# Moving norms, step sizes, a bias table and loads inside a two-block sequence model on one core

## What is computed

```python
h = rms_norm(x, norm_g[l]); proj = h @ w_in[l]
z, xbc, dt_raw, lru_gate, lru_x, q, gate_logits = jnp.split(proj, SPLIT_POINTS, axis=-1)
xbc = jax.nn.silu(causal_dwconv(xbc, ssd_conv_w[l], ssd_conv_b[l]))
dt = jax.nn.softplus((dt_raw + ssd_dt_bias[l]).astype(jnp.float32))
mem_n = rms_norm(mem, mem_norm_g[l])           # keys and values of the memory attention
# second block: x = x + rmsnorm(mixer(rmsnorm(x, pre_norm[i])), post_norm[i]) for S5, SWA, MLA, SGU
bias = rel_bias[t5_bucket(jnp.maximum(dist, 0))]   # SWA only
```

## Time and profile before

| what | us |
|---|---|
| median of three timed runs (2287.07 to 2291.01) | 2290.78 |
| the profiled execution, its own time | 2285.02 |
| span of the profiled execution | 2283.2 |
| PE busy in it | 2060.8 |
| DVE, ACT, POOL busy | 1276.0, 873.3, 483.9 |

### The profile page before, as it was taken

The page is one execution under the profiler, slowest core; times in us unless marked ns, Lnnn a source line. Parts: engine busy times, 40 slices in busy tenths (PEclk is TensorE's granted clock), DMA queues, the critical chain, the costliest instruction groups (busy, mean ns, idle before and its releaser), DMA issues.

```text
span 2283.2 us, 25052 instructions
## 1 busy us (share of the span) xinstructions
PE 2060.8 (90%) x10096; PEld 1601.8 (70%) x10096; DVE 1276.0 (56%) x1807; ACT 873.3 (38%) x1262; POOL 483.9 (21%) x394
## 2 busy tenths in 40 slices
PE   5899998999999998999998888979879988898986
PEld 3687776678757887768797666857667755567865
DVE  5887666634729342455445534466476365637383
ACT  4225555422159223422332243335532344444332
POOL 3961221132238600423300100011001001100001
PEclk9899999999999999999999999989989999999998
DMA  2242111133422432624545622621122301113311
GB/s 115 82 155 99 38 38 37 65 106 110 143 92 93 148 111 88 226 82 130 176 131 137 149 74 74 116 89 42 70 79 74 110 20 37 37 58 119 110 56 55
DMA packets 53138, 215.26 MB, mean 94 GB/s; under 512 B 6048, under 2 KB 23104, under 8 KB 32672
## 3 DMA queue, kind: packets, MB, share of 16 engines
q1 hardware_dynamic: 22896, 162.54, 20.4%
q0 software_dynamic: 9488, 35.94, 5.6%
q10 hardware_dynamic: 20640, 15.19, 3.0%
HBM read 196.14 MB, written 17.50 MB: 94 GB/s over the span
## 4 chain that ended last, share of the span: by engine, by line
PE 61%; DVE 11%; ACT 6%; issue 4%; DMA 1%; ACTq 1%; POOL 0%; DVEq 0%; PEldq 0%; POOLq 0%
PE bank L480 17%; PE bank L481 17%; PE bank L482 17%; PE bank L479 2%; DVE ring_low L442 1%; ACT ring_high L437 1%; PE bank L3038 1%; ACT swa_s L2945 1%; PE bank L3065 1%; PE bank L1854 1%; ACTq L2325 1%; DVE lru_x L1768 1%; DVE swa_s L2883 1%; DVE gated_low L2745 1%; PE bank L613 1%
## 5 line engine op out<-in xcount | busy, mean ns | idle before, releaser
L480 PE MATMUL bank<-h_high,ring_high 128*128 128x512 f32 x1248 | 507.5, 407 | 50.6 <-DVE h_low L1282 22.2
L442 DVE TENSOR_TENSOR ring_low<-ring,ring_high 128x2048 fp32r<-128x2048 f32 x136 | 333.2, 2451 | 362.7 <-ACT ring_high L437 362.6
L481 PE MATMUL bank<-h_low,ring_high 128*128 128x512 f32 x1248 | 494.6, 396 | 0.0
L482 PE MATMUL bank<-h_high,ring_low 128*128 128x512 f32 x1248 | 493.2, 395 | 0.0
L437 ACT ACTIVATE ring_high<-ring 128x2048 fp32r<-128x2048 f32 x145 | 277.3, 1913 | 533.4 <-PE bank L482 497.9
L480 PEld LDWEIGHTS bank<-h_high,ring_high 128*128 128x128 f32 x1248 | 239.9, 192 | 127.7 <-issue 48.0
L481 PEld LDWEIGHTS bank<-h_low,ring_high 128*128 128x128 f32 x1248 | 240.0, 192 | 52.0 <-issue 3.9
L482 PEld LDWEIGHTS bank<-h_high,ring_low 128*128 128x128 f32 x1248 | 239.5, 192 | 51.8
L480 PE MATMUL bank<-gated_high,ring_high 128*128 128x512 f32 x256 | 106.0, 414 | 25.1 <-issue 18.3
L442 POOL TENSOR_TENSOR ring_low<-ring,ring_high 128x2048 fp32r<-128x2048 f32 x9 | 43.1, 4791 | 305.3 <-ACT ring_high L437 305.3
L481 PE MATMUL bank<-gated_low,ring_high 128*128 128x512 f32 x256 | 103.7, 405 | 0.0
(11 more groups left out here) (518 smaller groups left out, 3963.9 us busy)
## 6 DMA issues: line engine op xcount, KB each, us to landing
ring<-slabs SPq DMA_DIRECT2D x149, 1024.0 KB, 4.8
s_outputs<-s_ca POOLq DMA_DIRECT2D x4, 1152.0 KB, 4.9
x<-xT SPq DMA_DIRECT2D x2, 2048.0 KB, 8.3
s_b<-s_br POOLq DMA_DIRECT2D x8, 512.0 KB, 4.3
s_rows<-s_powers POOLq DMA_DIRECT2D x16, 256.0 KB, 6.6
s_inputs<-s_w POOLq DMA_DIRECT2D x8, 512.0 KB, 3.1
s_ck<-s_outputs POOLq DMA_DIRECT2D x1, 4096.0 KB, 23.5
s_wv<-s_inputs ACTq DMA_DIRECT2D x8, 512.0 KB, 4.9
```

The source lines that it names most:

```text
L442: dve.tensor_tensor(self.ring_low[:, s % RING, :], self.ring[:, s % RING, :], self.ring_high[:, self.splits_before[s] % AHEAD, :].bitcast( ...
L480: pe.matmul(out, w[0], x[0], start=start, stop=False)
L481: pe.matmul(out, w[0], x[1], start=False, stop=False)
L482: return pe.matmul(out, w[1], x[0], start=False, stop=stop)
```

## The change

Eight pieces of work move; no arithmetic is dropped. First norm: squares are gathered on DVE and summed by one pair of matmuls, right when x has landed; the two first slab splits go between its steps; scaling, high and low parts go one k behind another on ACT and DVE alone, without POOL. The S5 coefficients move behind the norm. The dt tile and the first three tiles are made with k outermost in four banks. The step sizes' `log1p_small` moves behind tile 4's convolution and the sums behind tile 9's. The memory norm runs beside the q tiles. `load_kernels` moves up in `stage_s5_u`, and `evac_z` goes to the end of its own step. `swa_bias` moves into S5's `gated_output`. In the MLA entry `total` takes the pinned bank 7.

```diff
-    add("dt", tile("w_in", KD, np.r_[span(C_DT, SSD_H), np.full(P - SSD_H, -1)]))
-    for m in range(24):
+    for k in range(KD):
+        add("xbc", [("w_in", span(k * P), np.r_[span(C_DT, SSD_H), np.full(P - SSD_H, -1)])])
+        add("xbc", [("w_in", span(k * P), span(C_XBC + m * P)) for m in range(3)])
+    for m in range(3, 24):
...
 stage_load, scalar
-            act.wait_ge(cols.sem, cols.base + 16)
-            s5_act(act)
+            act.wait_ge(C.consts.sem, C.consts.at(0))
+            act.activation(C.eps8[:, 6:7], C.eps[:], ACT.Sqrt)
             act.wait_ge(loaded.sem, loaded.base + 16)
-            for s in range(AHEAD):
-                C.make_high(act, s)
...
 stage_xbc, vector
-            norm.on_dve(dve)
-            norm.finish(dve)
+            for i in range(KD):
+                norm.gather(dve, i)
+            C.make_low(dve, 0)
+            norm.parts_on_dve(dve, {3: lambda dve: C.make_low(dve, 1)})
+            norm.done(dve, KD - 1)
+            for _, use in ends:
+                C.split_low(dve, use)
+            s5_dve(dve)
...
+            C.split_low(dve, us[-1])
...
-                C.split_low(dve, u)
+                if i >= 3:
+                    C.split_low(dve, u)
+                if i == 4:
+                    step_sizes()
+                if i == 9:
+                    step_sums()
 stage_xbc, scalar
-            norm.on_act(act)
-            C.split_high(act, dt[0])
+            for i in range(KD):
+                norm.square(act, i)
+            C.make_high(act, 0)
+            norm.root_on_act(act)
+            C.make_high(act, 1)
+            norm.highs_on_act(act)
+            for _, use in ends:
+                C.split_high(act, use)
+            s5_act(act)
+            C.split_high(act, us[-1])
...
 Norm, new
+    def parts_on_dve(self, dve, between={}):
...
+        scale(0)
+        for i in range(n):
+            if i + 1 < n:
+                scale(i + 1)
+            dve.wait_ge(self.highs.sem, self.highs.at(i))
+            dve.tensor_tensor(self.pair.tile(i)[1], self.tmp[i], self.pair.tile(i)[0].bitcast(F32), ALU.subtract)\
+                .then_inc(self.parted.sem, 1)
+            if i in between:
+                between[i](dve)
...
 stage_gemm (beside=mem_norm in the q stage; on PE: sum_total after tile 4)
+                if beside and i < 4:
+                    beside.square(act, 2 * i)
+                    beside.square(act, 2 * i + 1)
+                if beside and i == 4:
+                    beside.root_on_act(act)
+                if beside and i == 5:
+                    beside.highs_on_act(act)
...
+                if beside and i == 4:
+                    beside.parts_on_dve(dve)
...
 stage_s5_u, scalar
                 if half == 1:
+                    act.wait_ge(kept.sem, kept.base + 16)
+                    for b in range(2):
+                        loads.load_kernels(act, b)
                     C.split_high(act, us[-1])
...
 stage_s5_scan, vector
-            evac_z(0)
...
-                if s + 1 < NB:
-                    C.split_low(dve, z[s + 1][0])
-                    evac_z(s + 1)
+                    if s > 0:
+                        C.split_low(dve, z[s][0])
+                    evac_z(s)
...
 swa_bias(C, L, free), now a side of S5's gated_output
     def pool_part(pool):
+        C.full(pool, free)
...
-    return Side({3: product}, pool=pool_part, act={3: copy}, dve_last=lambda dve: dve.wait_ge(s.sem, s.base + 32))
+    L.bias_laid = s
+    return Side({1: product}, pool=pool_part, act={1: copy})
 stage_swa, vector
+            dve.wait_ge(L.bias_laid.sem, L.bias_laid.base + 32)
...
 branch_mla
+    total = C.take_given(7)
     qn = Norm(C, latents[:6], lambda i: C.col("q_norm", i), 768, C.take_given(7), pair=QP, early=True)
```

More of the change, by code:

```diff
@@ L686, in stage_xbc @@
     nc = C.nc
-    dt = C.take_tile(KD)
-    tiles = [C.take_tile(KD) for _ in range(24)]
+    us = [C.take_bank() for _ in range(4)]
+    blocks, ends = [], []
+    for k in range(KD):
+        use = us[-1]
+        if k < KD - 1 and C.block_no % SLAB + 4 >= SLAB:
+            C.midway += 1
+            use = SlabSpent(C.midway)
+            ends.append((k, use))
+        blocks.append(C.take_blocks(4, use))
+    tiles = [(u, None) for u in us[1:]] + [C.take_tile(KD) for _ in range(21)]
+    s5_act, s5_dve = s5_coefficients(C)
     tables = Tables(C, L, items)
@@ L708, in _ @@
             seen = set()
-            norm.on_pe(pe)
-            C.gemm(pe, dt, C.H.tiles(KD), seen, ready=lambda k: norm.done(pe, k))
-            for t in tiles:
+            norm.sum_total(pe)
+            for u in us:
+                C.open(pe, u)
+            for k in range(KD):
+                norm.done(pe, k)
+                for u, (s, i) in zip(us, blocks[k]):
+                    C.wait_slab(pe, s, seen)
+                    mm = C.product(pe, C.bank[u.b][:], C.block(s, i), C.H.tile(k), k == 0, k == KD - 1)
+                    if k == KD - 1:
+                        mm.then_inc(C.bank_full[u.b], 1)
+                if k in dict(ends):
+                    mm.then_inc(C.slab_spent, 1)
+            for t in tiles[3:]:
                 C.gemm(pe, t, C.H.tiles(KD), seen)
@@ L1106, with __init__ @@
 class Norm:
-    def __init__(self, C, src, g, dim, bank, root=0, pair=None, keep=False, add=None, early=False, after=None, w=T, total=2, prior=None, split=False):
+    def __init__(self, C, src, g, dim, bank, root=0, pair=None, keep=False, add=None, early=False, after=None, w=T, total=2, prior=None, split=False, alone=False):
         self.C, self.src, self.g, self.dim, self.u = C, src, g, dim, bank
@@ L1127, in __init__ @@
             self.highs = C.reserve("highs", n)
-        if (pair is not None or add is not None) and not split:
+        if (pair is not None or add is not None) and not split and not alone:
             self.last_steps()
@@ L1354, in times_root, with stage_entry @@
         return evac
-def stage_entry(C, entry, nt, evac, engine="scalar", by_token=True, then=None, stats=(), side=None):
+def stage_entry(C, entry, nt, evac, engine="scalar", by_token=True, then=None, stats=(), side=None, total=None):
     side = side or Side()
@@ L2462, in _ @@
                         loads.load_outputs(act, b)
-            act.wait_ge(kept.sem, kept.base + 16)
-            for b in range(2):
-                loads.load_kernels(act, b)
     return loads, [us for us, _, _ in halves], first_z
```

163 lines of the change are left out of this document (93 added, 70 removed).

## The result

Median 2256.36 us (2253.57 to 2264.15, four runs) against 2288.93 (2286.05 to 2291.01) for the kernel before on the same chip: ratio 0.9865, 95% interval 0.9848 to 0.9881. That is 32.6 us less by the medians; the span of the profiled execution fell by 28.8 us, to 2254.4. The forecast was 38.5 us, 2252.

A forecast was written before the change was run, and what follows sets the result against it. PE, busy 90% of the span, was taken as the bound, so time is gained only where it waits or runs at low clock. Terms 8.5 + 11.5 + 5.5 + 12 - 7 + 8 = 38.5 us off median 2290.8 give 2252, range 2236 to 2271.

The forecast's parts named there:

- the xbc stretch gives all back: Rival, 15%: slow slab split beside POOL and tables 5 us late leave parts 1 and 2 only 0 to 3; 2260.
- 1. start, first h matmul: First norm: earlier squares and sums let the first h matmul start at 24.7 instead of 34.36, 9.6 us earlier.
- 1 and 2, at the states: Start and step sizes up to stage_ssd: 9.5 us gained by tile 9, about 1 lost to POOL's tables; 8.5 (3 to 11).
- 3. memory norm: Norm beside the q tiles: memory keys start at 895.5 instead of 903.33; 11.5 us gained (9 to 14).
- 4. S5 loads and copies: S5 branch: kernel loads moved up and z copies moved later shorten PE's waits; 5.5 us gained (2 to 9).
- 5. bias table, gain at the scores: SWA scores: bias ready some 50 us ahead, so DVE's and PE's waits for it go; 12 us gained.
- 5. bias table, loss at S5's output: S5's gated output: the 3 MB write delays slab 99 and the norm's sum; 7 us lost (0 to 9).
- 6. MLA total: MLA entry: tile 5's bank is free, so PE's 4.96 us wait and low clock go; 8 us gained (5 to 8).
- a stall above 15 us: Sign of being wrong: the step sizes' stall in the xbc stretch exceeds 15 us.
- the bias write at a place with less slack: Sign of being wrong: the moved bias write hits a place with less slack than assumed.
- The step sizes' stall: xbc stretch: the old 10 us wait comes back as about 11.5 us at tile 9, with 2.8 us of low clock.
- the forecast case (2240 to 2262): Whole kernel: time lands between 2240 and 2262 us, given 61%.

The follow-up runs named there:

- e5: The changed kernel with POOL's last table of stage_xbc (outputs 1) moved to the LRU stage: 2245.4 us, ratio 0.981 to the kernel before.
- e9: The changed kernel with the memory norm put back behind the q tiles, step by step: 2270.0 us, ratio 0.9925 to the kernel before.
- e10: The changed kernel with load_kernels and evac_z back where they were: 2254.6 us, ratio 0.9859 to the kernel before.
- e8: The changed kernel with swa_bias back in the SWA entry: 2260.0 us, ratio 0.9886 to the kernel before.
- e4: The changed kernel with the 3 MB bias write cut into eight pieces, each waited for: 2247.4 us, ratio 0.9817 to the kernel before.
- e11: The changed kernel with total taking the next bank again in the MLA entry: 2264.1 us, ratio 0.989 to the kernel before.
- e2: The changed kernel with log1p_small and the sums cut into nine pieces behind splits from tile 4 to 20: 2254.2 us, ratio 0.9848 to the kernel before.
- e1: The changed kernel with the S5 coefficients computed in stage_load while x is in flight: 2257.0 us, ratio 0.9843 to the kernel before.
- e3: The changed kernel with both early S5 coefficients in stage_load and the step sizes in nine pieces: 2246.4 us, ratio 0.9813 to the kernel before.

## Why the prediction was right, and where it was not

The forecast was 38.5 us less, the medians give 32.6, the spans 28.8. The sum held within 10 us, in part by luck: one term, the xbc stretch, came 6.1 us short at the states, and terms 3 and 4 gave 4.2 more than forecast. The time alone does not tell the forecast from a rival either: 2256.4 is 4.4 us above 2252 and 3.6 below the 2260 of "the xbc stretch gives all back". Term by term: the forecast; then the two traces, as the change of the lead over the stretch (the lead is 9.2 at h, 2.4 at the states, -2.7 at the end of the q tiles, 11.4 at the start of the S5 branch, and then as in the table above); then the run that undid or cured it:

| term | forecast | traces | run |
|---|---|---|---|
| 1. start, first h matmul | 9.6 | 9.2 | |
| 1 and 2, at the states | 8.5 | 2.4 | e5: 11.0 held back |
| the same, read at the end of the q tiles | 8.5 | -2.7 | |
| 3. memory norm | 11.5 | 14.1 | e9: 13.6 |
| 4. S5 loads and copies | 5.5 | 7.1 | e10: -1.8, not settled |
| 5. bias table, gain at the scores | 12 | 11.9 | e8: 13.1 |
| 5. bias table, loss at S5's output | -7 | -8.9 | e4: 9.0 |
| 6. MLA total | 8 | 7.8 | e11: 7.8 |

**1. The start** came as worked out: 25.20 against 24.7.

**2. The step that failed** is the sentence "The end of this stretch costs some back: ... After, 187 against 186: about 1." I moved POOL's chain by its later start alone, added 5 us for the landing, and found DVE there at 186. The start was right (50.22 against 50.7), and so was DVE (184.8). But the chain is 139.8 us long after, from 50.22 to the issue at 190.01, against 131.2 before (44.52 to 175.68), and the write lands 5.9 us behind its issue: at 195.9 instead of 187. PE's lead of 12.2 us at the end of its tiles was more than the 9.5 forecast; the end of the stretch then cost 9.8 instead of about 1. Of the 8.6 us that the chain grew, 7.7 are POOL's waits for its own DMAs. There are five in each kernel, one after another:

```profile
71.71 0.20 POOL L2159 MEMSET rot<- 128x32 f32 x2 [2.81 <-DMA s_kernels<-s_zero]
...
125.74 0.71 POOL L2187 DMA_DIRECT2D s_c<-s_c  x1 [8.85 <-DMA s_rotations<-rot]
```

before, and after

```profile
78.84 0.21 POOL L2239 MEMSET rot<- 128x32 f32 x2 [7.68 <-DMA s_kernels<-s_zero]
...
138.86 0.71 POOL L2267 DMA_DIRECT2D s_c<-s_c  x1 [10.90 <-DMA s_rotations<-rot]
```

At the first of them PE stood still before (62 to 72) and no slab was in flight. After, a slab is issued at 70.76, within a microsecond of POOL's write at 70.04; the slab takes 7.5 us instead of 4.8 and the write's wait is 7.68 instead of 2.81. The two issues (KB each, us to landing), where the write alone took 3.9 before:

```profile
ring<-slabs SPq DMA_DIRECT2D x1, 1024.0 KB, 7.5
s_kernels<-s_zero POOLq DMA_DIRECT2D x1, 448.0 KB, 8.8
```

The other four waits are 8.85, 2.58, 4.18 and 6.01 us before, and 10.90, 4.29, 7.29 and 1.98 after. Slabs are in flight beside some of these transfers in both kernels, but not beside the same ones. The last wait shrank: before, a slab was issued together with its transfer (at 151.37 and 151.35), after, the slab came 2 us behind it. The five add to 24.4 us before and 32.1 after. The first one is the steady part: 7.6 to 8.3 us in e2, e4, e5 and e8 to e11, whose POOL work up to there is unedited. The rest moves from run to run: in the six kernels with this stretch unedited (the changed one, e4, e8 to e11) the chain is 135.0 to 141.4 us, and in e4 DVE waits only 3.69 us for the last write. I had written that POOL and DVE slow each other and kept 0 to 5 for it; that POOL's first write would meet a slab which before was not there is what I left out.

The rival "the xbc stretch gives all back" is what happened in this stretch, by its second mechanism (tables late), not by its first: most of L444's splits took 2.3 us and the slowest 3.53, not 4. Its price for parts 1 and 2 (0 to 3) fitted the 2.4 at the states. Neither of the prediction's two signs of being wrong, a stall above 15 us or the bias write at a place with less slack, was what came.

The step sizes' stall itself was put at 11.5 us at tile 9 and is 8.62: the chain took 11.4 us where I had 12 to 14, and began 1.1 us earlier. e2 shows that this term had no weight in the changed kernel: take the stall away, and the time is the same, since DVE and PE both wait for the table.

From the states to the end of the q tiles another 5.1 us went. I can't assign them: the same stretch, unedited, scatters over 6 us in the other kernels, and kernels with a long stop ahead of it (e2, 697.3; e8, 694.2) don't differ from those without (e4, 698.6; e5, 694.2).

**3. Memory norm.** PE's stops around it fell from 2.88 + 3.69 + 3.92 to 2.50, for slab 63's low part, which the forecast named with 1 to 4. The other 6.1 us are between the keys and the next branch, more than the forecast's allowance for the clock.

**4. S5.** The two mechanisms are in the rows: third transposes without their wait, and outputs 7 waiting for kernel loads (4.96 us, named, put at 2.8). The size is open.

**5. Bias table.** Both halves held, within 2 us. The rows decided between two rules here. The changed kernel's slab issued at 1373.53, 5 us into the 3 MB write, moved nothing for 13 us and took 22.5. By queue (packets, MB, share of the 16 engines; q0 carries POOL's write, q1 the slabs), from 1374 to 1387 and from 1387 to 1403:

```profile
q0 software_dynamic: 279, 1.29, 95.6%
...
q0 software_dynamic: 330, 1.44, 66.1%
q1 hardware_dynamic: 302, 2.21, 32.8%
```

In e4 the slab issued in the middle of a piece an eighth as long took 6.6 us, and its 1.05 MB moved between 1391 and 1397. The Trainium skill ("DMA: Bandwidth & Descriptors", section "Queues, rings and completion order") has each DMA engine take turns between its queues packet by packet. By that rule, the trace does not agree for the first 13 us: with turns taken, the slab would have moved from the start and, by the prediction's estimate, been there in about 10 us. Why it stood is not shown.

**6. MLA total.** As forecast: the wait of 4.96 and the clock behind it.

The chances: faster was given 93%, and it is faster by 1.35%; the time lies in the forecast case (2240 to 2262), given 61%.

One reading at the head of the prediction was wrong, without weight in the sum: PE's waits add to 203 us, not 173, and the longest single one is not the 12.0 but 18.2 us, ahead of the first norm's sum (total us, times, longest):

```profile
PE bank L1148 <- ACT sq L1141: 21.1, 2, 18.2
```

## What to carry to other kernels

When a stall is removed, list everything that ends after it in the same stage, also on the engine nobody waits for, and recompute each chain with the transfers that the earlier start brings in: here POOL's last table landed 9 us later than a shift of its start showed. A stall that is the second longest path costs nothing (e2) until the longest is gone, so undo one cause at a time and then all together: e1 and e2 alone gave nothing by the medians, together (e3) they gave 10 us. A large write that is early enough by tens of microseconds can be sent in small pieces, each waited for, and then stops hurting the loads beside it.

## What the runs showed of the hardware

DVE steps with both inputs in SBUF can stretch when POOL works on wide tiles; steps that read a PSUM bank did not. Three polynomial steps (32x512) took 2.10, 5.43 and 8.50 us, by what POOL did; two scans 0.72 and 5.22; seven steps 4.96 and 8.98. A TENSOR_SCALAR with its one input in SBUF took 2.02 us in e1 and 0.41 in the changed kernel, while the RECIPROCAL ahead took 3.34 in both. The three convolution steps, which read a bank, took 2.31 or 2.32 us in every row read, with POOL busy or idle. POOL pays too: in e3 its operation over 128x1152 at 107.05 took 4.31 us beside DVE's slab split (3.56 us from 105.68 instead of 2.28), the one ahead of it 2.27. The Trainium skill ("SBUF — State Buffer", section "SBUF: two separate sides") calls the ports that DVE and POOL share a lock, held for a whole instruction, for DVE steps with two SBUF inputs. By that rule, the traces agree: in e3 the three steps end at 111.90, 115.00 and 117.66, each 0.5 us after one of POOL's operations ends (111.36, 114.45 and 117.13).

The other is the write of e4: 384 KB pieces took 5.5 to 6.2 us each, with 5.8 to 6.5 us from issue to issue, and the slabs beside them lost 0.2 to 1.7 us; one write of 3072 KB took 35.1 us and cost the slabs behind it 17.6, 13.3 and 5.5 us (22.5, 18.2 and 10.4 against 4.9).
